# Rotary queries from one product and a permutation of its copy, with all weights requested at once

## What the reference computes

```python
q = (rms_norm_2(cq, q_norm_w) @ w_q_up).reshape(b, l, 16, 64 + 32)     # cq has 384 channels
return q[..., :64], q[..., 64:]

def rotate_half_axial(x):
    def rh(t):
        a, b = jnp.split(t, 2, axis=-1)
        return jnp.concatenate([-b, a], axis=-1)
    xr, xc = jnp.split(x, 2, axis=-1)
    return jnp.concatenate([rh(xr), rh(xc)], axis=-1)

def apply_rope_2(x, cos, sin):
    return xf * cos + rotate_half_axial(xf) * sin
```

## Time and profile before

| | |
|---|---|
| median of 3 runs | 5525.56 us (5514.93, 5533.5, 5525.56) |
| the profiled execution | 5525.75 us |
| its span, first to last instruction | 5524.0 us |
| mean granted TensorE clock | 0.859 of 2.4 GHz |
| busy: PE, weight loads, DVE, ACT, POOL | 79%, 59%, 52%, 34%, 11% |
| first and last instruction of the stage query_rope | about 2926.9 and 2996.6 us |

### The profile page before, as it was taken

One profiled execution on the slowest core, in us unless ns is written; L12 is line 12 of the kernel. 1 busy time (PEld: TensorE's weight loads), 2 busy tenths in 40 slices (PEclk: granted clock), 3 DMA queues, 4 the chain that ended last, 5 costly groups with the idle time before them and its releaser, 6 DMA issues. The chain is left out here.

```text
span 5524.0 us, 56250 instructions
## 1 busy us (share of the span) xinstructions
PE 4350.9 (79%) x21480; PEld 3270.0 (59%) x21480; DVE 2888.4 (52%) x4273; ACT 1861.8 (34%) x3198; POOL 617.6 (11%) x858
## 2 busy tenths in 40 slices
PE   6758868678885984647876999998673868899998
PEld 4644557566664563536662565555562657688777
DVE  3454456564545545565553445443555755466545
ACT  3322342323432243232341333332322434334333
POOL 0001012210000101120001121210003600011100
PEclk7968887779897996767897999999786979999999
DMA  4000013213400000000411000002100044211134
GB/s 146 16 19 0 8 66 131 81 66 118 143 16 19 1 19 16 8 5 24 141 33 31 4 4 7 4 1 92 46 1 2 1 156 149 69 55 52 46 130 145
DMA packets 173532, 285.88 MB, mean 52 GB/s; under 512 B 43402, under 2 KB 98698, under 8 KB 173268
## 3 DMA queue, kind: packets, MB, share of 16 engines
q1 hardware_dynamic: 172516, 282.07, 15.2%
q0 software_dynamic: 608, 0.08, 0.1%
q10 hardware_dynamic: 144, 0.15, 0.0%
HBM read 257.01 MB, written 25.26 MB: 51 GB/s over the span
## 5 line engine op out<-in xcount | busy, mean ns | idle before, releaser
L307 DVE TENSOR_TENSOR x_low<-buf_a,x_high 128x1280 fp32r<-128x1280 f32 (+4 forms) x336 | 358.2, 1066 | 652.6 <-ACT x_high L290 651.7
L290 ACT CAST x_high<-buf_a 128x1280 fp32r<-128x1280 f32 (+4 forms) x336 | 310.0, 923 | 746.2 <-PE ps L330 627.1
L328 PE MATMUL ps<-x_high,w_high 128*128 128x256 f32 (+1 forms) x1344 | 498.0, 371 | 80.2 <-DVE w_low L311 78.3
L941 ACT ACTIVATE pt<-ps 128x512 f32<-128x512 f32 (+1 forms) x488 | 289.6, 594 | 745.6 <-PE ps L884 744.0
L894 PE MATMUL ps<-pt,v 128*128 128x512 f32 (+1 forms) x976 | 505.2, 600 | 0.0
L329 PE MATMUL ps<-x_low,w_high 128*128 128x256 f32 (+1 forms) x1344 | 492.0, 366 | 0.0
L330 PE MATMUL ps<-x_high,w_low 128*128 128x256 f32 (+1 forms) x1344 | 488.0, 363 | 0.0
L965 DVE TENSOR_REDUCE mx<-ps 128x1 f32<-128x1280 f32 (+1 forms) x200 | 289.8, 1449 | 343.2 <-PE ps L851 341.7
L3027 PE MATMUL ps<-w_high,x_high 128*128 128x512 f32 x896 | 370.0, 413 | 110.2 <-DVE w_low L2900 65.1
L3028 PE MATMUL ps<-w_low,x_high 128*128 128x512 f32 x896 | 363.3, 405 | 0.0
L3029 PE MATMUL ps<-w_high,x_low 128*128 128x512 f32 x896 | 362.4, 404 | 0.0
(11 more groups left out here) (388 smaller groups left out, 8816.2 us busy)
## 6 DMA issues: line engine op xcount, KB each, us to landing
w<-in_w_out SPq DMA_DIRECT2D x26, 2048.0 KB, 7.9
w<-in_w_mod SPq DMA_DIRECT2D x24, 2048.0 KB, 8.2
w<-in_w_down SPq DMA_DIRECT2D x15, 2048.0 KB, 7.8
w<-in_w_in SPq DMA_DIRECT2D x12, 2048.0 KB, 10.4
w<-in_w_up SPq DMA_DIRECT2D x22, 1024.0 KB, 7.6
w<-in_w_in SPq DMA_DIRECT2D x16, 1024.0 KB, 5.0
x<-in_x SPq DMA_DIRECT2D x16, 512.0 KB, 3.5
scratch_x<-x SPq DMA_DIRECT2D x16, 512.0 KB, 5.3
```

The lines of the kernel that those rows point to most:

```text
L290: act.copy(xh[i % NX][:, 0:s["tn"]], x_of(s)).then_inc(x_high, 1)
L307: dve.tensor_tensor(xl[i % NX][:, 0:s["tn"]], x_of(s), xh[i % NX][:, 0:s["tn"]].bitcast(F32), ALU.subtract).then_inc(x_low, 1)
L328: pe.matmul(g["out"], lhs[0][:, :], rhs[0][:, :], start=(s["kk"] == 0), stop=False)
L941: act.activation(pt[g % NPT][:, 0:w["nq"]], ps[:, 4 + g % 2, 0:w["nq"]], ACT.Exp, scale=scale).then_inc(exped, 1)
```

## The change

The swapped weights go. PE makes the plain product only (three matmuls a block); ACT copies it from its bank into `plain`, and a fourth matmul of a 128 x 128 permutation matrix `rope_swap` with this copy gives the swapped product. DVE multiplies the plain product from its bank by the cosines once the copy is made, and the permuted one by the sines. Plain products go round three banks (0 to 2), permuted ones round two (4, 5); `plain`, `t1` and `t2` are doubled. PE makes the plain product of the next block ahead of the permutation of this one. All weights are requested at once, in three transfers of 128 rows of 2 KB each (256 KB), ahead of the permutation matrix (64 KB) and the tables. The blocks go over the groups first and the halves second. The tables move from the tail layout to the other, the permutation matrix to the tail.

```diff
 def query_rope(k, cqT, qr, lay, lay2):
-    w = [lay(f"wqr{i}", [P, 3, P]) for i in range(2)]
-    tab = lay2("rope_fm", [P, 2, LAT])
-    t1 = lay("t1", [P, HALF])
-    t2 = lay("t2", [P, HALF])
+    NB = LAT // HALF
+    w = lay("wqr", [P, 3, 4, P])
+    swap = lay2("rope_swap", [P, P])
+    tab = lay("rope_fm", [P, 2, LAT])
+    plain = [lay(f"plain{i}", [P, HALF]) for i in range(2)]
+    t1 = [lay(f"t1{i}", [P, HALF]) for i in range(2)]
+    t2 = [lay(f"t2{i}", [P, HALF]) for i in range(2)]
+    blocks = [(g, b) for b in range(NB) for g in range(4)]
     with nc.Block() as block:
         @block.sync
         def _(sp):
+            for c in range(3):
+                sp.dma_start(w[:, c, :, :], d["wq_rope"][c * P:(c + 1) * P, :].rearrange("p (g n) -> p g n", n=P)
+                             ).then_inc(w_in, 16)
+            sp.dma_start(swap[:, :], d["rope_swap"]).then_inc(tab_in, 16)
             for i in range(2):
                 sp.dma_start(tab[:, i, :], d["rope2_fm"][i]).then_inc(tab_in, 16)
-            for g in range(4):
-                for i, s in enumerate((w_in0, w_in1)):
-                    if g >= 1:
-                        sp.wait_ge(ready, 4 * g)
-                    sp.dma_start(w[i][:, :, :], d[("wq_rope", "wq_rope_sw")[i]][:, g * P:(g + 1) * P].rearrange(
-                        "(c p) n -> p c n", p=P)).then_inc(s, 16)
             k.ws.load_until(sp, k.ws.taken)
 
         @block.tensor
         def _(pe):
-            for g in range(4):
-                pe.wait_ge(w_in0, 16 * (g + 1))
-                pe.wait_ge(w_in1, 16 * (g + 1))
-                for b in range(2):
-                    j = 2 * g + b
-                    if j >= 2:
-                        pe.wait_ge(done, j - 1)
-                    for i in range(2):
-                        for c in range(3):
-                            mm = pe.matmul(ps[:, 2 * (j % 2) + i, :], w[i][:, c, :], cqT[:, c, b * HALF:(b + 1) * HALF],
-                                           start=(c == 0), stop=(c == 2))
-                        mm.then_inc(ready, 1)
+            pe.wait_ge(w_in, 48)
+
+            def products(j):
+                g, b = blocks[j]
+                if j >= 3:
+                    pe.wait_ge(first_half, j - 2)
+                for c in range(3):
+                    mm = pe.matmul(ps[:, j % 3, :], w[:, c, g, :], cqT[:, c, b * HALF:(b + 1) * HALF],
+                                   start=(c == 0), stop=(c == 2))
+                mm.then_inc(ready, 1)
+
+            products(0)
+            for j in range(len(blocks)):
+                if j + 1 < len(blocks):
+                    products(j + 1)
+                if j == 0:
+                    pe.wait_ge(tab_in, 48)
+                if j >= 2:
+                    pe.wait_ge(second_half, j - 1)
+                pe.wait_ge(copied, j + 1)
+                pe.matmul(ps[:, 4 + j % 2, :], swap[:, :], plain[j % 2][:, :], start=True, stop=True).then_inc(swapped, 1)
+
+        @block.scalar
+        def _(act):
+            for j in range(len(blocks)):
+                act.wait_ge(ready, j + 1)
+                if j >= 2:
+                    act.wait_ge(swapped, j - 1)
+                act.copy(plain[j % 2][:, :], ps[:, j % 3, :]).then_inc(copied, 1)
 
         @block.vector
         def _(dve):
-            dve.wait_ge(tab_in, 32)
...
+            dve.wait_ge(tab_in, 48)
+            for j, (g, b) in enumerate(blocks):
+                cols = slice(b * HALF, (b + 1) * HALF)
+                dve.wait_ge(copied, j + 1)
+                if j >= 2:
+                    dve.wait_ge(turned, j - 1)
+                dve.tensor_tensor(t1[j % 2][:, :], ps[:, j % 3, :], tab[:, 0, cols], ALU.mult).then_inc(first_half, 1)
+                dve.wait_ge(swapped, j + 1)
+                dve.tensor_tensor(t2[j % 2][:, :], ps[:, 4 + j % 2, :], tab[:, 1, cols], ALU.mult).then_inc(second_half, 1)
+                dve.wait_ge(first_half, j + 1)
+                dve.wait_ge(second_half, j + 1)
+                dve.tensor_tensor(qr[:, g, cols], t1[j % 2][:, :], t2[j % 2][:, :], ALU.add).then_inc(turned, 1)
```

More of the change, by code:

```diff
@@ L1597, in query_rope @@
     nc, ps, d = k.nc, k.ps, k.d
-    w = [lay(f"wqr{i}", [P, 3, P]) for i in range(2)]
-    tab = lay2("rope_fm", [P, 2, LAT])
-    t1 = lay("t1", [P, HALF])
-    t2 = lay("t2", [P, HALF])
-    tab_in, w_in0, w_in1, ready, used, done, chain = sems = k.sems(
-        "tables_in", "w_plain_in", "w_swapped_in", "ready", "w_used", "turned", "dve_chain")
+    NB = LAT // HALF
[5 more added lines that the diff above has]
+    t2 = [lay(f"t2{i}", [P, HALF]) for i in range(2)]
+    tab_in, w_in, ready, copied, swapped, turned, first_half, second_half = sems = k.sems(
+        "tables_in", "weights_in", "products_ready", "plain_copied", "swapped", "turned", "first_half", "second_half")
+    blocks = [(g, b) for b in range(NB) for g in range(4)]
     with nc.Block() as block:
@@ L3245, in positions @@
         return [np.concatenate(dft(n, n ** -0.5)).astype(np.float32)]
+    swap = (r[:, None] == r[None, :] // 16 * 16 + (r[None, :] + 8) % 16).astype(np.float32)
     half_cos, half_sin = (a[:LAT // 2 + 1, :LAT // 2 + 1].astype(np.float32) for a in dft(LAT, LAT ** -0.5))
@@ L3267, in constants @@
     return dict(
-        ident=np.eye(P, dtype=np.float32), tri=tri, scan_select=select, level_masks=masks, dft_channels=ch.astype(np.float32),
+        ident=np.eye(P, dtype=np.float32), rope_swap=np.ascontiguousarray(swap), tri=tri, scan_select=select, level_masks=masks, dft_channels=ch.astype(np.float32),
         dft_ctx=positions(CTX)[0], dft_half=np.concatenate([half_cos[:LAT // 2], half_sin[:LAT // 2]]),
@@ L3279, in layouts @@
     rope = wq[:, :, NOPE:]
-    swap = np.concatenate([np.arange(8, 16), np.arange(8), np.arange(24, 32), np.arange(16, 24)])
     c = np.ascontiguousarray
-    return dict(wq_nope=c(wq[:, :, :NOPE]).reshape(QL, -1), wq_rope=c(rope).reshape(QL, -1),
-                wq_rope_sw=c(rope[:, :, swap]).reshape(QL, -1), wk_nope=c(wkv[:, :, :NOPE]).reshape(KVL, -1),
+    return dict(wq_nope=c(wq[:, :, :NOPE]).reshape(QL, -1), wq_rope=c(rope).reshape(QL, -1), wk_nope=c(wkv[:, :, :NOPE]).reshape(KVL, -1),
                 wv=c(wkv[:, :, NOPE:]).reshape(KVL, -1))
```

## The result

The changed kernel takes 5489.67 us (median of 7 runs, 5483.98 to 5505.15) against 5529.69 us before (7 runs, 5514.93 to 5538.83). The ratio is 0.9933 with an interval of 0.9917 to 0.9948, that is 37 us less, 29 to 46. Forecast were 5492.5 us, 33 less, with a range of 5481 to 5508. The median of the kernel before rose by 4.1 us from its first three runs to all seven, so the two absolute numbers (5492.5 and 5489.7) lie nearer together than the two differences do.

The account below looks back on a forecast made before the run. The stage, on the path between barriers, was taken as bound by PE's work, clock and weight waits. Terms 13.7 + 9.9 + 0.5 + 6.2 + 2.1 + 0.6 = 33.0 us gave 5492.5 us from 5525.56, range 5481 to 5508.

Parts of the forecast that it names:

- point 6: DVE at the stage's end: only sine product and sum left behind PE, no cosine product, 0.6 us less.
- Less for PE: PE's records in the stage: 96 become 64 at 0.429 us each, 13.7 us less.
- No waits between groups: PE's pauses for weights between bursts: 9.9 us go, and 0.5 us of drains before them.
- The clock: PE's low-clock stretches in bursts two to four go, 6.2 us less; the first stays at 5.8 us.
- The start: Stage's first transfers: weights lead the queue and land 4.4 us after first issue, 2.1 us sooner.
- The copy: ACT's copy ahead of each permutation: hidden behind the next block's product, 0 us, with 6.7 us as the other end.
- The barrier behind the last sum: Stage's end: next stage taken to start 1.84 us after the last sum; the remaining effects counted at nothing.
- Rival A: PE waits at each permutation because the copy comes late, exposing 6.7 us: kernel at 5499 us; chance 6%.
- Rival B: PE's clock stays low for all 64 records through small pauses, 24.3 us more: kernel at 5517 us; chance 6%.
- Rival C: Gain given back between 3800 and 4600 by a lower mean clock; at 0.75 the kernel takes 5545 us; chance 3%.
- Rival D: PE still pauses every two blocks, for another engine, as long as for weights: gain 16.4, kernel 5509 us; chance 3%.

Follow-up runs that it names:

- requests_only: Kernel before with both plain and swapped weights requested at once ahead of the tables, products as before: stage 55.3 us, ratio 0.997.
- perm_only: Permutation in place of swapped weights, but one weight buffer and a request per group as in the kernel before: stage 42.0 us, ratio 0.9935.
- tables_first: Changed kernel with tables and permutation matrix requested ahead of the weights: stage 41.9 us.
- no_ahead: Changed kernel with the next block's product issued behind this block's permutation, so PE waits for ACT's copy: stage 45.8 us.
- serial: Changed kernel with product, copy, permutation and DVE's sum in series before the next block's product: stage 61.9 us, ratio 0.9982.
- early: Changed kernel with weights, matrix and tables requested in the stage before, into free space: stage 32.2 us, ratio 0.9923.
- early_both: Changed kernel with this stage's inputs requested a stage earlier, and the first two head pairs' attention weights requested within this stage: ratio 0.9918, repeated 0.9924.

## Why the prediction was right

The forecast was right in its sign, its size and its mechanism; the stage lost 32.3 us by the profile against 33.0 in the sum. That these agree within 0.7 us is luck in part: misses of 0.7 to 1.0 us stand on both sides, and two profiles of each kernel give anything from 30.5 to 33.0. Two things the sum had not right: the end of DVE's work (point 6), and, without effect on the total, what the requests contribute (points 2 and 3).

1. *Less for PE*, 13.7: 64 records at 0.429, as forecast. requests_only, which keeps the 96, needs 13.6 us more from PE's first product on (47.1 against 33.5).
2. *No waits between groups*, 9.9 and 0.5: no idle time in the burst. As an effect of the requests this holds only in part: perm_only shows that the permutation alone halves the pauses.
3. *The clock*, 6.2: one low stretch, 4.4 us where I kept 5.8; 0.7 us better, inside the bounds. perm_only and requests_only each have one low stretch too, so either part alone takes the others away. The term itself is not sharp: the low stretch of the second burst before was 6.1 us in one profile and 3.0 in the other, which is 1.5 us of time.
4. *The start*, 2.1: the first product came 5.0 us after the first request, not 4.4, so 1.4 measured from the entry (5.85 us against 7.29); in the second profile it was 4.2 us. tables_first shows the order served, and confirms the 7.7 us for everything with 7.4. This agrees with the ring order that the Trainium skill gives (DMA: Bandwidth & Descriptors, Queues, rings and completion order).
5. *The copy*, 0: no permutation waited. The end of the range, 6.7, was met by no_ahead with 6.9, though by a cost per wait that was too small and a gain at the end that was left out.
6. *DVE*, 0.6 at the end: this is the term that was wrong. I had only sine product and sum behind PE. In fact the last two permutations run back to back (the row of four records), the sum of block 6 is still in DVE when block 7's permutation ends at 2963.08, and block 7's cosine product stands behind that sum. My own statement on the order, that a cosine product ends 2.1 us after the permutation of the block before, gives this: 2961.05 + 1.02 + 2.13 = 2964.20, which is 1.1 us behind PE's end. I didn't apply it to the last block. From PE's end to the start of the last sum it is 1.82 us, where it was 1.44 (2994.48 to 2995.92): 0.4 lost, 1.0 off the forecast.
7. The barrier behind the last sum was 0.2 shorter (1.62 us from its start, 1.84 before).

33.0 + 0.7 - 0.7 - 1.0 + 0.2 = 32.2.

*Rival A* is priced and excluded. *Rival B*, by which small pauses keep the clock down, fell: with one pause a block of 0.7 us, or one of 1.7 us in two blocks, the clock stayed at 1.00. In serial two of seven later products came at the low clock. What the Trainium skill describes (TensorE: Matmul & The Clock Gate, A second HAM failure mode: psum-queue depth-cycling) is one bf16 kernel that pauses briefly between groups and whose clock swings; I had made a rule of it, and of swings a clock low throughout, which is more than it says. Only serial shows such swings here, and no kernel a clock that stays low through the stage. *Rival C*, a gain given back behind the stage, fell too: 2525 to 2528 us lie behind it in every kernel with the attention unchanged, and the differences of the stage, -32.3, -29.7, -16.3, -9.8 and -39.5, each lie in the interval of the whole kernel's, which is 10 to 17 us wide. *Rival D* fell with points 2 and 5.

What stays open: the ratio says 37 us, in both comparisons, the stage says 32.3. The interval, from 29, holds both. The entry to the stage moves by up to 21 us between executions, and two profiles of each kernel don't settle 5 us of it.

## What to carry to other kernels

Where stages are separated by barriers, cut the trace at the barriers: the stage's own length repeated within 2 us here (0.7 us in the changed kernel), while the time ahead of it moved by 21 with the same code. So parts worth 3 us can be told apart in one or two profiles, where ten executions of the whole leave an interval of over 10 us. A product that can be made from another by a permutation costs two records in place of six, if the next block's product is issued ahead of it to cover the copy. Pauses of 3.2 to 3.4 us cost twice here, by themselves and by the clock behind them, three of 1.7 us only once; two cures of the same pauses don't add up. The first transfer of a stage is the pause that is left, and it goes by requesting it in the stage before; by the stage's length that was worth 6.5 to 7.2 us, which the whole times can neither confirm nor exclude.

## What the runs showed that I had not expected

The permutation alone, with one buffer and a request per group, is within 2.6 to 3.3 us of the full change (42.0 against 39.4 and 38.7 us): its first product starts 2.4 us after the first request and not 5.0, which pays for half of its three pauses of 1.7 us. The first group's weights in a small request ahead of the rest should have both advantages; it was not tried.

The clock at the start of a burst went with the idle time ahead of it: after 1.75 us (early) it stood at 2.4 GHz from the first record, after 6 to 9 us it was at 1.2 GHz for 4.4 us (changed) to 5.8 us. These are a few cases, and a burst can also begin at the full clock and lose it while PE works: the fourth burst of the kernel before has 0.93 in its first 1.5 us (2982.2 to 2983.7) and 0.51 behind that the earlier trace rows, and the attention of early_both, after 3.34 us of idle time, has 1.00 up to 2965.0 and 0.57 from there to 2969.0. So the burst's first records don't show what the pause ahead of it costs. In the attention of the changed kernel the clock was still at the low level 11 us after PE's start, in early_both it was not (0.51 against 0.85 in the windows of the two kernels below, in this order; the second profile of each shows the same). But that it stays low for so long is no effect of the change: the kernel before has 0.74 in such a window in one profile (3001.4 to 3012.8) and 0.50 for 11 us in the other (2994.9 to 3006.0).

```profile
2970.40:2982.10 11.70, 9.52 (x12) 3.50 (x12) 3.56 (x5) 1.89 (x4) 0.00 (x0) 0.51 0.05 15
```

```profile
2963.60:2975.00 11.40, 8.02 (x16) 3.29 (x17) 7.10 (x8) 3.05 (x6) 1.32 (x2) 0.85 0.00 0
```
